# The sample's weighted sums of values on four 32-column strips of the TensorE array

## The reference

```
p_cmp = masked_softmax(s, d_cmp >= 0)
o_cmp = einsum('bkgtn,bnkd->btkgd', p_cmp, vc)            # 255 compressed values
o_sel = einsum('bkgqm,bkqmd->bqkgd', p, vg)               # 4096 cached values, most weights zero
o_win = einsum('bkgqm,bmkd->bqkgd', p, kv[:, :, 1])       # the last 512 values
o = gates[:, :, 0] * o_cmp + gates[:, :, 1] * o_sel + gates[:, :, 2] * o_win
```

## Time and profile before

| | us |
|---|---|
| median of 3 runs | 3194.33 |
| lowest, highest | 3194.32, 3202.76 |
| span of the profiled execution | 3193.5 |
| TensorE matmuls busy, in that span | 2825.2 (88%) |
| TensorE weight loads busy | 2243.3 (70%) |
| VectorE busy | 1059.6 (33%) |
| ScalarE busy | 657.4 (21%) |
| mean granted TensorE clock | 0.899 |

### The profile page before, as it was taken

How to read it: one execution, slowest core, us unless ns; L and a number is a source line. 1 busy time by engine, 2 the same in 40 slices (tenths; PEclk the granted TensorE clock), 3 DMA queues, 4 the chain that set the end, 5 groups by cost and what they waited for, 6 DMA issues and landing times. The chain is left out here.

```text
span 3193.5 us, 40852 instructions
## 1 busy us (share of the span) xinstructions
PE 2825.2 (88%) x14496; PEld 2243.3 (70%) x14496; DVE 1059.6 (33%) x2571; ACT 657.4 (21%) x1514; POOL 226.7 (7%) x228
## 2 busy tenths in 40 slices
PE   6997999699698799999869889996978987999996
PEld 4876777466585588888658767765657765888885
DVE  1823555344543201000128244554444322100002
ACT  0023444223310100000011244442232102000001
POOL 0500000000030100000105000000002101000000
PEclk8997999799696899999979979997987878999998
DMA  6214555143001222222052165532420012222220
GB/s 189 67 46 147 176 185 171 51 116 96 2 21 45 66 77 71 76 69 67 1 144 66 41 200 173 164 122 81 121 62 1 21 47 86 73 67 76 69 53 28
DMA packets 334996, 274.00 MB, mean 86 GB/s; under 512 B 52865, under 2 KB 330562, under 8 KB 334458
## 3 DMA queue, kind: packets, MB, share of 16 engines
q1 hardware_dynamic: 300072, 247.38, 26.1%
q10 hardware_dynamic: 34770, 24.55, 2.6%
HBM read 262.01 MB, written 18.17 MB: 88 GB/s over the span
## 5 line engine op out<-in xcount | busy, mean ns | idle before, releaser
L370 PE MATMUL psum<-xT,up_ring 128*128 128x272 f32 x2048 | 473.7, 395 | 21.7 <-PEq L161 21.7
L370 PEld LDWEIGHTS psum<-xT,up_ring 128*128 128x128 f32 x2048 | 391.6, 191 | 104.4 <-issue 23.1
L370 PE MATMUL psum<-ff,HT 128*128 128x272 f32 x1536 | 356.5, 395 | 4.2 <-PEq L161 4.2
L370 PEld LDWEIGHTS psum<-ff,HT 128*128 128x128 f32 x1536 | 294.0, 192 | 66.1 <-issue 5.0
L370 PE MATMUL psum<-xT,w_ring 128*128 128x272 f32 x1408 | 329.1, 397 | 5.2 <-PEq L161 4.0
L370 PEld LDWEIGHTS psum<-xT,w_ring 128*128 128x128 f32 x1408 | 270.8, 193 | 63.4 <-issue 4.7
L1019 PE MATMUL psum<-chunks,W 128*128 128x512 f32 x512 | 240.4, 631 | 10.6 <-DVE chunks L1141 10.6
L1141 DVE COPY chunks<-psum 64x256 f32<-64x256 f32 x512 | 215.1, 420 | 33.5 <-PE psum L998 26.2
L2143 DVE SCALAR_TENSOR_TENSOR xT<-xT,psum 128x544 f32<-128x544 f32 x32 | 23.1, 721 | 592.8 <-PE psum L370 592.8
L998 PE MATMUL psum<-cst,cache 128*128 128x128 f32 x1536 | 199.1, 283 | 20.7 <-DMA cache<-in_cache_nsa_kv 20.7
L998 PEld LDWEIGHTS psum<-cst,cache 128*128 128x128 f32 x1536 | 183.4, 150 | 29.8 <-DMA cache<-in_cache_nsa_kv 22.4
(11 more groups left out here) (415 smaller groups left out, 3283.6 us busy)
## 6 DMA issues: line engine op xcount, KB each, us to landing
cache<-in_cache_nsa_kv SPq DMA_DIRECT2D x512, 192.0 KB, 3.3
up_ring<-in_w_up SPq DMA_DIRECT2D x32, 1024.0 KB, 5.3
vsel<-in_cache_nsa_kv SPq DMA_DIRECT2D x384, 64.0 KB, 2.0
w_ring<-in_w_in SPq DMA_DIRECT2D x20, 1024.0 KB, 5.3
HT<-in_w_down SPq DMA_DIRECT2D x10, 2048.0 KB, 9.1
vsel<-in_cache_nsa_kv ACTq DMA_DIRECT2D x128, 64.0 KB, 2.2
HT<-in_w_out SPq DMA_DIRECT2D x8, 1024.0 KB, 5.9
yT<-in_w_down SPq DMA_DIRECT2D x4, 2048.0 KB, 12.3
```

The costliest lines, as they stand in the source:

```text
L370: last = pe.matmul(psum[0:w.shape[1], 2 * (t % 4) + h, 0:HALF], w, moving(k)[:, h * HALF:(h + 1) * HALF], start=(k == 0), stop=(k == kt - 1))
```

## The change

The 16 columns of a sequence are widened to 32 (those of the even and the odd sequence of a pair, so that 16 of the 32 result rows belong to a neighbour and are not used). Products go in turn to four results, at psum partitions 0 to 31, 32 to 63, 64 to 95 and 96 to 127 of the same bank, which are the four 32-column strips of the array: page product t to strip t mod 4. Each strip is an accumulation group of its own, opened by one of the first four products. ScalarE copies all 128 partitions to `o_s`, now 128 partitions high. At the end the eight turns of 16 rows become eight fp32 matmuls of 128 rows by 128 columns with a moving operand of 16 columns, `fold`, a table of ones that picks the sequence's own 16 rows out of each strip and adds the four strips. The table of constants grows by 32 columns (2165 to 2197).

No instruction changes its place: each engine issues the same instructions in the same order as before, and no wait is added or removed. Line numbers grow by 1 from L115 on.

```diff
+    t["fold"] = i[:, None] % 32 == np.arange(32)[None, :]
...
-    o_s = sb("o_s", [16, NB, P], ctx=ctx)
+    o_s = sb("o_s", [P, NB, P], ctx=ctx)
...
-                cols = slice(16 * b, 16 * b + 16)
-                o = psum[0:16, 6 + b % 2, 0:P]
+                cols = slice(32 * (b // 2), 32 * (b // 2) + 32)
+                o = [psum[32 * c:32 * c + 32, 6 + b % 2, 0:P] for c in range(4)]
...
-                    pe.matmul(o, S.pt_new[:, 0, cols], S.kv_s[:, 3 * P:4 * P], start=True, stop=False)
-                    pe.matmul(o, S.pt_new[:, 1, cols], S.kv_s[:, 5 * P:6 * P], start=False, stop=False)
+                    pe.matmul(o[0], S.pt_new[:, 0, cols], S.kv_s[:, 3 * P:4 * P], start=True, stop=False)
+                    pe.matmul(o[1], S.pt_new[:, 1, cols], S.kv_s[:, 5 * P:6 * P], start=True, stop=False)
                     for j in range(2):
                         m = P - j
-                        pe.matmul(o, S.pt_cmp[0:m, j, cols], S.vc[0:m, j, b, :], start=False, stop=False)
+                        pe.matmul(o[2 + j], S.pt_cmp[0:m, j, cols], S.vc[0:m, j, b, :], start=True, stop=False)
                     pe.wait_ge(s.window, 16 * b + 16)
                     for j in range(4):
-                        pe.matmul(o, S.st_win[:, j, cols], vwin[:, j, :], start=False, stop=False)
+                        pe.matmul(o[j], S.st_win[:, j, cols], vwin[:, j, :], start=False, stop=False)
...
-                    last = pe.matmul(o, S.st_sel[:, half * h + t, cols], vsel[:, h, t, :], start=False, stop=(h == 1 and t == half - 1))
+                    last = pe.matmul(o[t % 4], S.st_sel[:, half * h + t, cols], vsel[:, h, t, :], start=False, stop=(h == 1 and t >= half - 4))
...
-                last = pe.transpose(psum[:, 7, 16 * b:16 * b + 16], o_s[:, b, :], C["ident"][0:16, 0:16])
+                own = C["fold"][:, 16 * (b % 2):16 * (b % 2) + 16]
+                last = pe.matmul(psum[:, 7, 16 * b:16 * b + 16], o_s[:, b, :], own, start=True, stop=True)
...
-                act.copy(o_s[:, b, :], psum[0:16, 6 + b % 2, 0:P]).then_inc(s.s_copied, 1)
+                act.copy(o_s[:, b, :], psum[:, 6 + b % 2, 0:P]).then_inc(s.s_copied, 1)
```

## The result

The changed kernel takes 3238.9 us in the median of 4 runs (3236.58 to 3249.86) against 3198.55 us for the kernel before on the same chip: a ratio of 1.0135, with a 95% interval of 1.0111 to 1.0160. It is slower by 40 us, where 3175.7 us were forecast. The profiled span is 3236.9 us, 43.4 us more than before.

The account below looks back on a forecast made before the run. TensorE was taken to set the stage's end, with SyncE nearly as loaded at 18.5 us a block. Gains of 9.4 and 12.2 us, less 3 for the clock, made 18.6: 3175.7 us forecast, range 3166 to 3184.

Parts of the forecast that it names:

- What bounds the kernel: Stage `att`: TensorE seems to set the end, but SyncE's 18.5 us a block is nearly as loaded and limits the gain.
- The price of a product: Page products on changing strips: 0.14 us each instead of 0.218, a saving of 0.078 us.
- The start and the tail: Stage's ends, per layer: SyncE starts sequence 1 earlier, gaining 2.8 us; the last 16 products end sooner, gaining 2.4 us.
- The fold: End of the stage: 16 records take 1.8 us in place of 0.5, costing 1.3 us more.
- The middle, and the clock: Middle blocks: SyncE's waits vanish, 5.5 us in the first layer, 8.3 in the second; clock charged 3 us for both.
- The clock gives it back: Rival, blocks 1 to 4: overlap works but idle time keeps the clock at 0.50; about 3191 us, chance 0.11.
- Draining strips: Rival, page products: each strip change costs up to 0.09 us and streams don't overlap; 3241 us, chance 0.09.
- The gain at the full clock: Both layers' stages: 21.6 us gained before 3 us charged for the clock, leaving 18.6 us.

Follow-up runs that it names:

- e9: The kernel before, with SyncE fetching 8 of its 12 pages of a part from sequence 1 on (output wrong): 3169.4 us, ratio 0.9931.
- e11: The kernel before, with SyncE fetching 10 pages of a part instead of 12 and ScalarE 6, in two pieces: 3172.2 us, ratio 0.9941.
- e7: The changed kernel with four strips in turn for the last sequence only, eight products at a time per strip in the others: 3189.2 us, ratio 0.9978.
- e1_runs: The changed kernel with page products going to one strip eight at a time and the window's to strip 0: 3197.0 us, ratio 1.0005.
- e3: The changed kernel with sequences 0 and 1 as in e1_runs and sequences 2 to 7 on four strips: 3246.7 us, ratio 1.0155.
- e5: The changed kernel plus 3 filler products on one strip ahead of each third's page products: 3196.7 us, ratio 0.9978.
- e6: The changed kernel plus 5 filler products on one strip ahead of each third's page products: 3201.3 us, ratio 1.0009.
- e2: The changed kernel with page products alternating between two strips only, the window's likewise: 3226.1 us, ratio 1.0072.
- e4: The kernel before without its page products except the last of each third, waits and fetches kept (output wrong): 3183.9 us, one run.
- e12: e5 with 10 pages of a part fetched by SyncE and 6 by ScalarE, in two pieces: 3179.1 us, ratio 0.9951.

## Why the prediction was wrong

*What bounds the kernel.* Right. TensorE bounded sequences 3 to 6, and SyncE's 18.5 us a block were close under it and ahead of it in sequences 1 and 2: taking pages from it gained 0.7% with the products untouched (e9), and moving two of twelve gained 0.6% (e11).

*The price of a product.* Right in direction, mis-sized: 0.052 us at the full clock (e7) where the sum took 0.14. Not two but four streams run at once. The prediction had 0.06 as the lower end, and let the second record of a product hold up the next product; it doesn't. The page "TensorE: Matmul & The Clock Gate" of the Trainium skill, section "Part 3: Packing small matmuls", gives 2.38x for three strips; four gave 0.218 / 0.052 = 4.2x here. Its rule that weight loads overlap only across row groups was not borne out: the changed kernel's page products load all 128 rows of each strip and begin a record every 0.055 us, where one weight load takes 0.13 to 0.18 us. By the prediction's own terms 0.052 adds 2 x (12 x 0.088 + 12 x 0.176 + 16 x 0.088) = 9 us of gain, the wrong way for the result. (The 2.2 us a layer that it gives for the page's price are 2.5 by the same terms.)

*The start and the tail.* From the stage's first record to SyncE's first fetch for sequence 1 it is 644.22 - 622.5 = 21.7 us in the changed kernel, 644.89 - 620.4 = 24.5 before: 2.8 us earlier, as forecast, and in the second layer too. That the number fits is in part luck, since here the products saved more and the prompt's work between them was slower. The tail is there when the clock is up (e7: the last 16 products end 1.08 us after their pages land, 2.5 forecast); in the changed kernel it could not show.

*The fold.* 16 records in 1.93 us, nearly as forecast (1.8), for 8 in 0.64. In e1_runs, which has it too, no loss can be measured.

*The middle, and the clock.* This is the step that failed. The prediction charged "3 us for both layers, for waits of SyncE that come back", and gave a clock that costs more than the gain a chance of 0.02. Where 3 us were charged, the clock took away the 21.6 us of gain and 41.8 us more. The prediction looked at the idle time of TensorE (and at a wait of 2.29 us during which, not after which, the clock fell: it began at 2235.87, the fall is at 2236.9) and let 1.00 stand for the blocks of the earlier trace rows, where TensorE has no idle time. It didn't ask what TensorE streams while it is busy. The page products were what it did for 8.7 of 19 to 21 us a block, one stream at a time; overlapped, they are done in a quarter of that. What took their place is 184 us at 0.50 in each layer, in which the prompt's 12.5 us of a block (21.2 - 8.7) becomes about 24.2 (28.6 less 40 x 0.110). A block of 28.6 us is far over SyncE's 18.5, so the slack that was to absorb slow stretches didn't exist: it is 0.4 to 2.6 us a block at the full clock, and the blocks of sequences 3 to 6 at the half clock lie 5 to 10 us over SyncE's.

e1 shows that with next to no overlap there is no loss, e3 that the clock falls when the overlap begins, and e5 and e6 that added streaming brings it back with the strips unchanged.

*The rivals.* "The clock gives it back" named the right loss, with the wrong cause and far too small a price: it put the low clock down to idle time at each part, in blocks 1 to 4, and assumed three stretches of 13.7 us in a layer. There is one of 184, and in the blocks of sequences 2 to 6 within it TensorE has no idle time. "Draining strips" forecast the measured time almost exactly (3241 for 3238.9), by luck, and was wrong in its mechanism: records of different strips follow each other by less than 0.01 us. A time that fits is no proof; the spacing of the records in the first trace of the changed kernel settles it.

*The gain at the full clock* is not measured: no run has the changed products, the clock at 1.00 throughout and no fillers. The nearest, e5, gains 0.2% (0.06 to 0.38), where 0.6% was forecast, with fillers to pay for and 49 to 55 us at 0.50. The forecast took all of SyncE's waits but those ahead of sequence 1 as gone, while stretches at 0.50 went on causing them: 13.5 and 9.4 us in e5, where about 4 each were expected.

What stays open: by what measure of its activity TensorE keeps the clock, and so why it sometimes rises and sometimes falls in like work (e2, e4, e12), and whether e7's closing strips would add to e11; this was not run.

## What to carry to other kernels

Before packing or overlapping matmuls in a stage that TensorE bounds, ask which of them keep the granted clock up, and price the rest of the stage at the half clock too. Read the price where TensorE bounds: blocks that wait for pages anyway lost nothing at 0.50. A change that empties TensorE is safest in a place that little follows, as the last sequence here. And look for the queue that is nearly as loaded as the bounding engine, and for the few blocks in which it is ahead: moving two page fetches of twelve to another queue gained 0.6%, the best arrangement of the products 0.2%.

## What the runs showed of the hardware

fp32 matmuls with 32-column stationary operands on the four column strips run side by side: 0.218 us a product on one strip, 0.052 us in turn on four (e7), both at the full clock, and the weight loads keep up. Page products on four strips, with the prompt's work between them, kept the granted clock at 0.50 for 184 us in both layers, though the profile calls TensorE busy for 176 us of those: a high busy share in the profile is no sign that the clock will be granted. With 288 useless products more, the same kernel ran 1.6% faster (0.9978 against 1.0135 of the kernel before).
